# State-space scan of a decoder trunk: outputs channel-major in the two partition halves, with a cross-chunk decay matrix

## The chip, the cores and the metric

The kernel runs on one core of a Trainium2 chip. The metric is the device time of one execution in microseconds (us). The engines are TensorE (PE, with its weight loads as PEld), VectorE (DVE), ScalarE (ACT), GpSimd (POOL) and SyncE (SP), which issues the weight loads.

## The reference

The reference is a trunk of four pre-norm residual layers with 256 tokens of 1024 channels. Layers 0 and 3 mix tokens by latent attention, layer 1 by block attention, layer 2 by a Mamba-2 state-space mixer; each is followed by a squared-ReLU MLP. The change is in the mixer of layer 2, whose scan works in two chunks of 128 tokens:

```python
def ssd_scan(xh, dt, a, bm, cm):
    x_dt = chunks(xh * dt[..., None])
    a_cs = jnp.cumsum(chunks(dt * a), axis=2)
    ...
    cb = jnp.einsum('bclgn,bcsgn->bclsg', cc, bc)
    y_diag = jnp.einsum('bclsg,bclsgr,bcsgrp->bclgrp', cb, decay_in, x_dt)
    decay_out = jnp.exp(a_cs[:, :, -1:] - a_cs)
    states = jnp.einsum('bclgn,bclgr,bclgrp->bcgrpn', bc, decay_out, x_dt)
    ...
    y_off = jnp.einsum('bclgn,bcgrpn,bclgr->bclgrp', cc, prev, jnp.exp(a_cs))
    return (y_diag + y_off).reshape(B, S, *xh.shape[2:])
```

There are 32 heads of 64 channels in two groups of 16. `decay_in` is `exp(a_cs[l] - a_cs[s])` for s up to l, else 0. The output then gets the skip term, is gated by `silu(z)`, normalised per group and projected by `ssd_w_out`.

## The kernel before, in words

Every weight matrix is cut into units of up to 1 MB. SP fetches a unit into one of four slots (`raw`); ACT makes its rounded high part (`whi`, line 474) and DVE the rest (`wlo`, line 484). A product with a weight is three products of such parts (`mm3`, lines 501 to 503; in output projections lines 695, 696 and 699). `act_splits` and `dve_splits` say how far ahead of PE the splitting goes. Outputs of PE go to four PSUM banks in turn, handed out by `Jobs`: each job takes the next bank, and PE waits until the bank's previous user has been read. `acc` is four further banks for the output projections. Every engine executes its own list in the order of the code.

The mixer's stage (`pe_ssd`, `act_ssd`, `dve_ssd`, `pool_ssd`) has two parts. First ten convolution steps: PE projects 256 channels (`cv`), ACT copies them and starts the sum, DVE adds three taps (line 1471), ACT applies silu (line 1349); `xsT`, `BT` and `CT` hold the results channel-major. After step 4, `Btok` (the transposed B of chunk 0) and `cbm` (C times B, masked) are made. The scan loop then makes passes q = 0 to 4, of which 0 to 3 take eight heads each. In a pass PE:

- transposes `xsT` to token-major (`xT`, line 1295); DVE multiplies by dt (line 1543) into `xdt`, and by the decay to the chunk's end (line 1552) into `dxdt`;
- transposes the outputs of the pass before (`yT`, line 1304) back to channel-major, which DVE gates (`gate`, lines 1514 and 1520);
- projects two units of z (`z`, 2q and 2q+1), between them multiplies `Btok` by `dxdt` (`st`, line 1311), the state after chunk 0, copied to `prevT` by ACT;
- forms the products within chunks (`ydiag`, line 1273, called for both chunks), 16 products with `dec` as weights and 64 moving columns, and between them reads the state (`yo`, line 1316). ACT copies chunk 0's outputs to `y_sb`, DVE scales the state's part (line 1584) and adds (line 1590) for chunk 1;
- in some passes projects gated outputs (`pe_out`, units `so`): `out_units` gives so0 and so1 to pass 1, so2 and so3 to pass 2, so4 to so7 to pass 4.

`dec` is prepared one pass ahead: POOL fetches the cumulated sums of eight heads, spread over all partitions (`load`, line 1613), DVE subtracts each row's own sum (`diffs`, line 1484), ACT takes the exponential (`decays`, line 1383), DVE multiplies by `cbm` (`decay_cb`, line 1492). ACT holds one set of function tables at a time, so going from silu to the exponential and back costs a table load each.

Of the kernel before, what the change touches and what calls it, by code (L numbers as in the profile page):

```python
# [21 lines left out]
P = 128  # L22
# [80 lines left out]
def build(nc, A, out, stages):  # L103

    ctx = ExitStack()
    with ctx:
# [73 lines left out]
        tokv = sb("tokv", [P, 6, SSD_H])  # L180
# [42 lines left out]
        prevT = xn[:, 1, 512:1024]  # L223
        y_sb = junk[:].rearrange("p (c n) -> p c n", c=T)
        with ExitStack() as stage:
# [3 lines left out]
            Btok = sb("Btok", [P, SSD_G, P], F32, stage)  # L229
# [12 lines left out]
        if "ssd" in kinds:  # L242
            (ssd_loaded, upper_loaded, acs_stored, dt_abs, dt_exp, dt_u, dt_ln, dt_out, da_done, acs_done, dec_io,
             drows_done, conv_done, silu_done, dec_diff, dec_exp, dec_ready, dx_done, g_done, gsq_done, gadd_done,
             ghi_done, glo_done, gms_done, grstd_done, ssd_half, tokv_done) = (sem(n) for n in (
                 "ssd_loaded upper_loaded acs_stored dt_abs dt_exp dt_u dt_ln dt_out da_done acs_done dec_io "
                 "drows_done conv_done silu_done dec_diff dec_exp dec_ready dx_done g_done gsq_done gadd_done "
                 "ghi_done glo_done gms_done grstd_done ssd_half tokv_done").split())
# [119 lines left out]
        def plan_ssd(L):  # L368
# [4 lines left out]
            for n in range(10):  # L373
# [854 lines left out]
        DT, EXP, U, LN, DD, DEC, DTO, ACS = range(8)  # L1228

        def pe_ssd(te, j, L):  # L1230
# [12 lines left out]
            for n in range(10):  # L1243
                if n:
                    proj(("cv", n))
                if n == 4:
                    te.wait_ge(dt_out, 1)
                    te.wait_ge(acs_done, 1)
                    te.wait_ge(dec_io, 2)
                    ps = open_job(te, "tokv")  # L1250
                    for i, (row, c) in enumerate(((DTO, 0), (DTO, 1), (ACS, 0), (ACS, 1), (DEC, 0), (DEC, 1))):
# [11 lines left out]
                    ps = open_job(te, "Btok")  # L1263
                    for g in range(SSD_G):
                        mm = nc.tensor.transpose(ps[:, g * P:(g + 1) * P], BT[:, g, tok(0)], ident[:])
                    mm.then_inc(ready("Btok"), 1)
            job_copied(te, "Btok")
            def ydiag(q, c):
                te.wait_ge(dec_ready, 2 * q + c + 1)
                job_copied(te, ("xT", q, c))  # L1270
                ps = open_job(te, ("yd", q, c))
                for hh in range(8):
                    mm = nc.tensor.matmul(ps[:, hh * SSD_HD:(hh + 1) * SSD_HD], dec[:, (2 * q + c) % 4, hh, :],  # L1273
                                          xdt[:, c, hh * SSD_HD:(hh + 1) * SSD_HD], start=True, stop=True)
                mm.then_inc(ready(("yd", q, c)), 1)
# [11 lines left out]
            for q in range(5):  # L1287
# [9 lines left out]
                if q:  # L1297
                    job_copied(te, ("yd", q - 1, 0))
                    job_copied(te, ("yd", q - 1, 1))
                    for u in range(2):  # L1300
                        ps = open_job(te, ("yT", q - 1, u))
                        for i in range(2):
                            for c in range(T):
                                mm = nc.tensor.transpose(ps[:, i * SEQ + c * P:i * SEQ + (c + 1) * P],
                                                         y_sb[:, c, (2 * u + i) * P:(2 * u + i + 1) * P], ident[:])
                        mm.then_inc(ready(("yT", q - 1, u)), 1)
# [515 lines left out]
```

## Time and profile before

| | before |
|---|---|
| median of 3 runs | 1401.88 us (1400.38 to 1404.24) |
| profiled execution: time, span | 1399.73 us, 1397.8 us |
| mean granted TensorE clock | 0.983 |
| PE busy | 1332.3 us (95%), 8604 records |
| DVE busy | 857.0 us (61%) |
| ACT busy | 668.0 us (48%) |
| POOL busy | 40.5 us (3%) |

The span runs from the first to the last instruction. The share of busy time is an average over stages; the scan stage lies at about 660 to 870 us of the span. A matmul of fp32 operands has two records in the trace, a transpose one. A record's duration includes the time in which the next one has started, so what a product costs in a dense run is the distance between starts. The granted clock is 1.00 at 2.4 GHz and 0.50 at 1.2 GHz.

### The profile page before, as it was taken

How to read it: one execution, taken by the hardware profiler on the slowest of the kernel's cores; microseconds unless marked ns; L12 is line 12 of the kernel's file. 1: busy time of each engine (PE TensorE's matmuls, PEld its weight loads, DVE VectorE, ACT ScalarE, POOL GpSimd, SP SyncE). 2: the span in 40 equal slices, each digit the busy share in tenths (PEclk: the TensorE clock that was granted, in tenths of full speed). 3: DMA queues.
4: the chain of work that ended last, by engine and by line, in shares of the span. 5: the costliest groups of instructions: out<-in, count | busy, mean ns of one | idle time of the engine just before them, and what ended most of it. 6: DMA issues, size and time to landing. Idle time of an engine off the chain costs nothing.

```text
span 1397.8 us, 20308 instructions
## 1 busy us (share of the span) xinstructions
PE 1332.3 (95%) x8604; PEld 1211.0 (87%) x8604; DVE 857.0 (61%) x1125; ACT 668.0 (48%) x834; POOL 40.5 (3%) x59
## 2 busy tenths in 40 slices
PE   5899999999999899999997999999999999899997
PEld 5788789999899799998897997999988898799996
DVE  4777665554564665555798686655556776565553
ACT  4455454443455454443765553544434545544442
POOL 2000000000000000000101110000000000000000
PEclk9899999999999999999998999999998999999999
DMA  8654165556554365552773443755535233375540
GB/s 255 159 151 150 61 226 182 188 196 188 160 172 151 130 231 195 186 181 90 230 238 104 136 155 127 247 181 181 186 116 197 98 123 122 129 236 190 181 151 31
DMA packets 147834, 231.06 MB, mean 165 GB/s; under 512 B 7651, under 2 KB 116493, under 8 KB 147744
## 3 DMA queue, kind: packets, MB, share of 16 engines
q1 hardware_dynamic: 144896, 221.66, 48.5%
q0 software_dynamic: 2848, 8.10, 2.7%
q8 instruction: 69, 1.13, 0.3%
q14 instruction: 21, 0.17, 0.0%
HBM read 227.08 MB, written 2.65 MB: 164 GB/s over the span
## 4 chain that ended last, share of the span: by engine, by line
PE 83%; DVE 9%; ACT 4%; issue 2%; DMA 2%; POOL 0%; SPq 0%; DVEq 0%; POOLq 0%; ACTq 0%
PE bank L501 14%; PE bank L503 14%; PE bank L502 14%; PE acc L695 11%; PE acc L696 11%; PE acc L699 11%; DVE wlo L484 3%; PE bank L829 3%; ACT whi L474 2%; PE bank L847 1%; PE bank L630 1%; DMA raw<-in_mla_w_in 1%; DMA raw<-in_mla_w_ukv 1%; PE bank L837 1%; PE bank L1273 1%
## 5 line engine op out<-in xcount | busy, mean ns | idle before, releaser
L484 DVE TENSOR_TENSOR wlo<-raw,whi 128x2048 fp32r<-128x2048 f32 (+2 forms) x209 | 467.6, 2246 | 206.4 <-ACT whi L474 206.3
L474 ACT ACTIVATE whi<-raw 128x2048 fp32r<-128x2048 f32 (+2 forms) x209 | 388.7, 1870 | 92.3 <-PE acc L699 82.9
L501 PE MATMUL bank<-hhi,whi 128*128 128x256 f32 x1448 | 416.2, 287 | 11.2 <-DVE hlo L574 7.1
L502 PE MATMUL bank<-hlo,whi 128*128 128x256 f32 x1448 | 412.4, 285 | 0.0
L503 PE MATMUL bank<-hhi,wlo 128*128 128x256 f32 x1448 | 412.4, 285 | 0.0
L501 PEld LDWEIGHTS bank<-hhi,whi 128*128 128x128 f32 x1448 | 279.4, 193 | 17.3 <-DVE hlo L574 9.0
L502 PEld LDWEIGHTS bank<-hlo,whi 128*128 128x128 f32 x1448 | 279.5, 193 | 3.3 <-issue 1.0
L503 PEld LDWEIGHTS bank<-hhi,wlo 128*128 128x128 f32 x1448 | 279.5, 193 | 0.2
L696 PE MATMUL acc<-wlo,uhi 128*128 128x512 f32 x512 | 200.0, 391 | 0.0
L695 PE MATMUL acc<-whi,uhi 128*128 128x512 f32 x512 | 199.6, 390 | 0.0
L699 PE MATMUL acc<-whi,ulo 128*128 128x512 f32 x512 | 159.1, 389 | 0.0
L778 ACT ACTIVATE relu<-bank 128x512 f32<-128x512 f32 x64 | 38.2, 597 | 213.3 <-PE bank L503 213.3
L699 PEld LDWEIGHTS acc<-whi,ulo 128*128 128x128 f32 x512 | 96.1, 188 | 20.4
L791 DVE TENSOR_TENSOR rsq<-relu 128x512 f32<-128x512 f32 x64 | 44.2, 691 | 112.1 <-ACT relu L778 112.1
L696 PEld LDWEIGHTS acc<-wlo,uhi 128*128 128x128 f32 x512 | 96.4, 188 | 18.1
L695 PEld LDWEIGHTS acc<-whi,uhi 128*128 128x128 f32 x512 | 96.4, 188 | 18.0
L794 DVE TENSOR_TENSOR ulo<-rsq,uhi 128x512 fp32r<-128x512 f32 x64 | 44.3, 693 | 50.5 <-ACT uhi L782 50.5
L782 ACT ACTIVATE uhi<-rsq 128x512 fp32r<-128x512 f32 x64 | 40.5, 632 | 64.4 <-DVE rsq L791 55.6
L695 PE MATMUL acc<-whi,ohi 128*128 128x512 f32 x160 | 63.9, 399 | 0.8 <-issue 0.8
L696 PE MATMUL acc<-wlo,ohi 128*128 128x512 f32 x160 | 62.6, 391 | 0.0
L501 PE MATMUL bank<-whi,hhi 128*128 128x256 f32 (+1 forms) x160 | 47.7, 298 | 10.5 <-DVE wlo L484 6.7
L529 ACT ACTIVATE hhi<-bank 128x512 fp32r<-128x512 f32 x32 | 18.7, 598 | 81.6 <-PE bank L630 81.5
(213 smaller groups left out, 1664.7 us busy)
## 6 DMA issues: line engine op xcount, KB each, us to landing
raw<-in_mlp_w SPq DMA_DIRECT2D x128, 1024.0 KB, 5.3
raw<-in_ssd_w_in SPq DMA_DIRECT2D x18, 1024.0 KB, 6.1
raw<-in_mla_w_o SPq DMA_DIRECT2D x16, 1024.0 KB, 5.0
raw<-in_mla_w_ukv SPq DMA_DIRECT2D x8, 1024.0 KB, 7.6
raw<-in_moba_w_qkv SPq DMA_DIRECT2D x16, 512.0 KB, 6.7
raw<-in_ssd_w_out SPq DMA_DIRECT2D x8, 1024.0 KB, 5.0
raw<-in_mla_w_uq SPq DMA_DIRECT2D x8, 768.0 KB, 7.4
raw<-in_mla_w_in SPq DMA_DIRECT2D x4, 1024.0 KB, 7.6
```

Of the source, the lines that this page charges most:

```text
L474: nc.scalar.activation(whi[:, s, :e], raw[:, s, :e], ACT.Copy).then_inc(w_hi_done[s], 1)
L484: nc.vector.tensor_tensor(wlo[:, s, :e], raw[:, s, :e], whi[:, s, :e].bitcast(F32), ALU.subtract).then_inc(w_split[s], 1)
L501: nc.tensor.matmul(ps, lhs[0], rhs[0], start=start, stop=False)
L502: nc.tensor.matmul(ps, lhs[0], rhs[1], start=False, stop=False)
L503: return nc.tensor.matmul(ps, lhs[1], rhs[0], start=False, stop=stop)
L695: nc.tensor.matmul(acc[t][half][:], lh, wh[:, k, n], start=first_unit and k == 0, stop=False)
L696: nc.tensor.matmul(acc[t][half][:], lh, wl[:, k, n], start=False, stop=False)
L699: mm = nc.tensor.matmul(acc[t][half][:], ll, wh[:, k, n], start=False, stop=last_unit and k == 1)
L782: nc.scalar.activation(uhi[:, c % 2].rearrange("p a b -> p (a b)"), rsq[:, c % 2, :], ACT.Copy).then_inc(uhi_done, 1)
L791: nc.vector.tensor_tensor(rsq[:, c % 2, :], relu[:, c % 2, :], relu[:, c % 2, :], ALU.mult).then_inc(usq_done, 1)
L794: nc.vector.tensor_tensor(ulo[:, c % 2].rearrange("p a b -> p (a b)"), rsq[:, c % 2, :], uhi[:, c % 2].rearrange("p a b -> p (a b)").bitca ...
L829: mm = nc.tensor.matmul(dst, q[:, tok(t)], k[:, 0:(t + 1) * P], start=n == 0, stop=n == len(parts) - 1)
```

## The change

The state is gone. For eight heads a third tile beside the two of `dec`, called `cross`, holds the decay from the end of chunk 0 to each token of chunk 1, `exp(a_cs)` of chunk 1, times `cbx`, which is C of chunk 1 by B of chunk 0. It lies in `junk`; POOL fetches its sums (`load_cross`), ACT takes the exponential (`cross_decay`), DVE multiplies by `cbx` (`cross_cb`). The products are turned round: `xdt` and `dxdt` are the weights, 64 columns of one head each, and `dec` and `cross` move past them, so the result is channel-major and needs no transposing. The two heads of a pair go to partitions 0 to 63 and 64 to 127 of the same bank, and the cross product is added to chunk 1's in PSUM. `gate` reads that bank. Removed are `Btok`, `st`, `prevT`, `yo`, `y_sb`, `yT` and their copies.

The order also changes. The first `diffs`, `decays` and `decay_cb` go into the convolution steps 5, 7 and 8, with the first cross tile. `split_early` and `split_late` say which units are split where. DVE makes `dxdt` ahead of the gates. A pass has six jobs instead of ten; so the bank of `y` 2q is taken again by `z` 2q+2, and the job `ss` takes a bank out of turn.

```diff
-        prevT = xn[:, 1, 512:1024]
-        y_sb = junk[:].rearrange("p (c n) -> p c n", c=T)
+        cross = junk[:].rearrange("p (h n) -> p h n", h=8)
...
-            Btok = sb("Btok", [P, SSD_G, P], F32, stage)
+            cbx = sb("cbx", [P, SSD_G, P], F32, stage)
...
-                    jobs.add("Btok")
+                    jobs.add("cbx")
             for q in range(5):
                 if q < 4:
                     jobs.add(("xT", q, 0))
                     jobs.add(("xT", q, 1))
-                if q:
-                    jobs.add(("yT", q - 1, 0))
-                    jobs.add(("yT", q - 1, 1))
-                if q < 4:
...
-                        if u == 0:
-                            jobs.add(("st", q))
-                    jobs.add(("yd", q, 0))
-                    jobs.add(("yo", q))
-                    jobs.add(("yd", q, 1))
+                    jobs.add(("y", 2 * q))
+                    jobs.add(("y", 2 * q + 1))
                 if q in (2, 4):
-                    jobs.add(("ss", q // 2 - 1))
+                    turn = jobs.last
+                    jobs.add(("ss", q // 2 - 1), bank=(turn + 2) % 4)
+                    jobs.last = turn
...
+        so_of = {L: {n: ("so", L, n) for n in range(8)} for kind, L, i in stages if kind == "ssd"}
+        split_early, split_late = {}, {}
+        for so in so_of.values():
+            split_early = {0: ("z", 3), 1: ("z", 4), 2: so[3], 3: so[5]}
+            split_late = {0: so[1], 1: ("z", 5), 2: ("z", 7), 3: so[7]}
...
-                    ps = open_job(te, "Btok")
+                    ps = open_job(te, "cbx")
                     for g in range(SSD_G):
-                        mm = nc.tensor.transpose(ps[:, g * P:(g + 1) * P], BT[:, g, tok(0)], ident[:])
-                    mm.then_inc(ready("Btok"), 1)
-            job_copied(te, "Btok")
-            def ydiag(q, c):
-                te.wait_ge(dec_ready, 2 * q + c + 1)
-                job_copied(te, ("xT", q, c))
-                ps = open_job(te, ("yd", q, c))
...
+                        mm = nc.tensor.matmul(ps[:, g * P:(g + 1) * P], BT[:, g, tok(0)], CT[:, g, tok(1)],
+                                              start=True, stop=True)
+                    mm.then_inc(ready("cbx"), 1)
+            def scan(n):
+                q = n // 2
+                ps = open_job(te, ("y", n))
+                for i in range(2):
+                    hh = [4 * (n % 2) + 2 * i + a for a in range(2)]
+                    ch = [slice(h * SSD_HD, (h + 1) * SSD_HD) for h in hh]
+                    dst = [ps[a * SSD_HD:(a + 1) * SSD_HD, i * SEQ:(i + 1) * SEQ] for a in range(2)]
+                    for a in range(2):
+                        nc.tensor.matmul(dst[a][:, tok(0)], xdt[:, 0, ch[a]], dec[:, (2 * q) % 4, hh[a], :],
+                                         start=True, stop=True)
+                    for a in range(2):
+                        nc.tensor.matmul(dst[a][:, tok(1)], xdt[:, 1, ch[a]], dec[:, (2 * q + 1) % 4, hh[a], :],
+                                         start=True, stop=False)
+                    for a in range(2):
+                        mm = nc.tensor.matmul(dst[a][:, tok(1)], dxdt[:, ch[a]], cross[:, hh[a], :],
+                                              start=False, stop=True)
+                mm.then_inc(ready(("y", n)), 1)
...
-                if q:
...
                 if q < 4:
                     proj(("z", 2 * q))
+                    proj(("z", 2 * q + 1))
+                    job_copied(te, ("xT", q, 0))
+                    job_copied(te, ("xT", q, 1))
                     te.wait_ge(dx_done, q + 1)
-                    ps = open_job(te, ("st", q))
-                    nc.tensor.matmul(ps[:], Btok[:, q // 2, :], dxdt, start=True, stop=True).then_inc(ready(("st", q)), 1)
-                    proj(("z", 2 * q + 1))
-                    job_copied(te, ("st", q))
-                    ydiag(q, 0)
-                    ps = open_job(te, ("yo", q))
-                    nc.tensor.matmul(ps[:], CT[:, q // 2, tok(1)], prevT, start=True,
-                                     stop=True).then_inc(ready(("yo", q)), 1)
-                    ydiag(q, 1)
+                    te.wait_ge(dec_ready, 2 * (q + 1))
+                    te.wait_ge(cross_ready, q + 1)
+                    scan(2 * q)
+                    scan(2 * q + 1)
...
+            def cross_decay(q):
+                act.wait_ge(cross_loaded, 16 * (q + 1))
+                nc.scalar.activation(cross, cross, ACT.Exp).then_inc(cross_exp, 1)
...
+                if n == 7:
+                    decays(0)
+                    cross_decay(0)
...
-            decays(0)
             for q in range(5):
+                if q == 0:
+                    act_splits(act, ("z", 0))
                 if 0 < q < 4:
                     for n in (2 * q - 2, 2 * q - 1):
                         gate_square(n)
                         gate_hi(n)
+                    cross_decay(q)
                 if q == 4:
                     gate_square(6)
                     gate_square(7)
-                    act_splits(act, ("so", L, 4))
                     gate_hi(6)
                     gate_hi(7)
                 if q < 4:
                     for u in range(2):
                         n = 2 * q + u
-                        act_splits(act, ("z", n), AHEAD - 1)
                         ps = job_ready(act, ("z", n))
...
                         if u == 0:
-                            ps = job_ready(act, ("st", q))
-                            nc.scalar.activation(prevT, ps[:], ACT.Copy).then_inc(freed(("st", q)), 1)
-                    ps = job_ready(act, ("yd", q, 0))
-                    nc.scalar.activation(y_sb[:, 0, :], ps[:], ACT.Copy).then_inc(freed(("yd", q, 0)), 1)
-                    act_splits(act, ("z", 2 * q + 1))
+                            act_splits(act, split_early[q], 0)
                 if q < 3:
                     decays(q + 1)
-                for n in out_units[q]:
-                    act_splits(act, ("so", L, n), AHEAD - 1)
+                if q < 4:
+                    act_splits(act, split_late[q], 0)
+            act_splits(act, ("so", L, 7), AHEAD - 1)
...
+            def cross_cb(q):
+                dve.wait_ge(cross_exp, q + 1)
+                nc.vector.tensor_tensor(cross, cross, cbx[:, q // 2, :].unsqueeze(1).to_broadcast([P, 8, P]),
+                                        ALU.mult).then_inc(cross_ready, 1)
...
+                if n == 5:
+                    diffs(0)
+                if n == 8:
+                    job_copied(dve, "cb")
+                    job_copied(dve, "cbx")
+                    decay_cb(0, 0)
+                    decay_cb(0, 1)
+                    cross_cb(0)
...
-                ps = job_ready(dve, ("yT", n // 2, n % 2))
+                ps = job_ready(dve, ("y", n))
...
-                        dve.wait_ge(dx_done, q)
+                        dve.wait_ge(*jobs.at["y", 2 * q - 1][1])
                     for c in range(T):
...
-                if q:
-                    gate(2 * q - 2)
-                    gate(2 * q - 1)
-                if q < 4:
                     job_copied(dve, ("xT", q, 0))
                     nc.vector.tensor_tensor(dxdt.rearrange("p (h d) -> p h d", h=8),
                                             xdt[:, 0, :].rearrange("p (h d) -> p h d", h=8),
                                             tokv[:, 4, hs].unsqueeze(2).to_broadcast([P, 8, SSD_HD]),
                                             ALU.mult).then_inc(dx_done, 1)
-                if q == 0:
-                    diffs(0)
-                    decay_cb(0, 0)
-                    decay_cb(0, 1)
-                if q == 4:
-                    dve_splits(dve, ("so", L, 4))
+                if q:
+                    gate(2 * q - 2)
+                    gate(2 * q - 1)
...
+                if 0 < q < 4:
+                    cross_cb(q)
                 if q < 4:
-                    dve_splits(dve, ("z", 2 * q), AHEAD - 1)
-                    dve_splits(dve, ("z", 2 * q + 1), AHEAD - 1)
+                    dve_splits(dve, split_early[q], 0)
                     if q < 3:
                         diffs(q + 1)
...
-                    if q < 3:
                         decay_cb(q + 1, 0)
                         decay_cb(q + 1, 1)
-                    dve_splits(dve, ("z", 2 * q + 1))
+                    dve_splits(dve, split_late[q], 0)
                 if q == 2:
                     mean_square(0)
                 if q == 4:
                     mean_square(1)
-                for n in out_units[q]:
-                    dve_splits(dve, ("so", L, n), AHEAD - 1)
-                if q == 4:
+                    dve_splits(dve, ("so", L, 7), AHEAD - 1)
...
-                        pool.wait_ge(*jobs.at["yd", q - 2, c][1])
+                        pool.wait_ge(*jobs.at["y", 2 * q - 3][1])
                     src = acs_dram[8 * q:8 * q + 8, tok(c)].unsqueeze(0).to_broadcast([P, 8, P])
                     pool.dma_start(dec[:, b], src).then_inc(dec_loaded[b], 16)
+            def load_cross(q):
+                if q:
+                    pool.wait_ge(*jobs.at["y", 2 * q - 1][1])
+                src = acs_dram[8 * q:8 * q + 8, tok(1)].unsqueeze(0).to_broadcast([P, 8, P])
+                pool.dma_start(cross, src).then_inc(cross_loaded, 16)
...
+            load_cross(0)
...
+                if n % 2 == 0 and n < 6:
+                    load_cross(n // 2 + 1)
+                if n in (0, 2):
+                    load(n // 2 + 2)
...
-                if n in (1, 3):
-                    load(n // 2 + 2)
```

On DVE, at the end of the convolution and up to the first gate of pass 1, the kernel before has this order (lines of the kernel before: 1471 convolution taps, 484 weight split, 1543 and 1552 `xdt` and `dxdt`, 1484 subtractions, 1492 `decay_cb`, 1514 gate):

```order
L1471 SCALAR_TENSOR_TENSOR cacc<-cvin,scol,cacc 128x256 x6
L1543 TENSOR_TENSOR xn<-bank,tokv 128x512 x2
L1552 TENSOR_TENSOR xn<-xn,tokv 128x512
L1484 TENSOR_SCALAR dec<-dec,tokv 128x128 x16
L1492 TENSOR_TENSOR dec<-dec,cbm 128x1024 x2
L484 TENSOR_TENSOR wlo<-raw,whi 128x2048
L1484 TENSOR_SCALAR dec<-dec,tokv 128x128 x16
L1584 TENSOR_TENSOR junk<-bank,tokv 128x512
L1590 TENSOR_TENSOR junk<-bank,junk 128x512
L1492 TENSOR_TENSOR dec<-dec,cbm 128x1024 x2
L484 TENSOR_TENSOR wlo<-raw,whi 128x2048
L1543 TENSOR_TENSOR xn<-bank,tokv 128x512 x2
```

The changed kernel has (line 1472 taps, 1493 `decay_cb`, 1498 `cross_cb`, 479 split, 1556 and 1561 `xdt` and `dxdt`, 1485 subtractions, 1527 gate):

```order
L1472 SCALAR_TENSOR_TENSOR cacc<-cvin,scol,cacc 128x256 x6
L1493 TENSOR_TENSOR dec<-dec,cbm 128x1024 x2
L1498 TENSOR_TENSOR junk<-junk,cbx 128x1024
L479 TENSOR_TENSOR wlo<-raw,whi 128x2048
L1472 SCALAR_TENSOR_TENSOR cacc<-cvin,scol,cacc 128x256 x6
L1556 TENSOR_TENSOR xn<-bank,tokv 128x512 x2
L1561 TENSOR_TENSOR xn<-xn,tokv 128x512
L479 TENSOR_TENSOR wlo<-raw,whi 128x2048
L1485 TENSOR_SCALAR dec<-dec,tokv 128x128 x16
L1493 TENSOR_TENSOR dec<-dec,cbm 128x1024 x2
L479 TENSOR_TENSOR wlo<-raw,whi 128x2048 x2
L1556 TENSOR_TENSOR xn<-bank,tokv 128x512 x2
```

The first pass's multiplies now stand ahead of the last convolution step, and one more split stands ahead of pass 1's `xdt`.

On PE, between the end of pass 0's second z unit and pass 1's first, the kernel before has 16 products of `dec` around the read of the state, then two kinds of transposes:

```order
L1273 MATMUL bank<-xn,dec 128x64 x8
L1316 MATMUL bank<-xn,CT 128x512
L1273 MATMUL bank<-xn,dec 128x64 x8
L1295 MATMUL bank<-ident,xsT 128x128 x8
L1304 MATMUL bank<-ident,junk 128x128 x8
```

In the changed kernel the same place holds 24 products with 64 output partitions, each pair for the two halves, and one kind of transposes (the three rows stand four times):

```order
L1279 MATMUL bank<-dec,xn 64x128 x2
L1282 MATMUL bank<-dec,xn 64x128 x2
L1285 MATMUL bank<-junk,xn 64x128 x2
...
L1307 MATMUL bank<-ident,xsT 128x128 x8
```

The list gives a product once though the trace has two records of it.

## Rows read from the trace of the kernel before

**Rows 1.** The page's part 1 (busy time by engine) and part 4 (the chain):

```profile
PE 1332.3 (95%) x8604; PEld 1211.0 (87%) x8604; DVE 857.0 (61%) x1125; ACT 668.0 (48%) x834; POOL 40.5 (3%) x59
PE 83%; DVE 9%; ACT 4%; issue 2%; DMA 2%; POOL 0%; SPq 0%; DVEq 0%; POOLq 0%; ACTq 0%
```

**Rows 2.** Timeline of PE: start us, us, engine, line, operation, [idle before, releaser]:

```profile
759.84 0.55 PE L501 MATMUL bank<-hhi,whi 128*128 128x256 f32 x1 [3.78 <-DVE xn L1543]
...
774.81 1.90 PE L1273 MATMUL bank<-xn,dec 128*128 128x64 f32 x16
776.54 1.08 PE L1316 MATMUL bank<-xn,CT 128*128 128x512 f32 x2
777.46 1.89 PE L1273 MATMUL bank<-xn,dec 128*128 128x64 f32 x16
...
790.16 1.04 PE L1295 MATMUL bank<-ident,xsT 128*128 128x128 f32 x8
...
797.66 1.02 PE L1311 MATMUL bank<-xn,Btok 128*128 128x512 f32 x2
...
798.64 0.28 PE L502 MATMUL bank<-hlo,whi 128*128 128x256 f32 x1
...
820.51 1.04 PE L1295 MATMUL bank<-ident,xsT 128*128 128x128 f32 x8
...
840.06 1.06 PE L1304 MATMUL bank<-ident,junk 128*128 128x128 f32 x8 [0.90 <-issue]
840.88 0.48 PE L695 MATMUL acc<-whi,ghi 128*128 128x512 f32 x1
```

**Rows 3.** Timeline of DVE, last convolution steps and first two turns:

```profile
728.42 2.71 DVE L1471 SCALAR_TENSOR_TENSOR cacc<-cvin,scol,cacc 128x256 f32<-128x256 f32 x6 [0.84 <-ACT cacc L1361]
...
736.81 1.28 DVE L1543 TENSOR_TENSOR xn<-bank,tokv 128x512 f32<-128x512 f32 x2
738.01 0.68 DVE L1552 TENSOR_TENSOR xn<-xn,tokv 128x512 f32<-128x512 f32 x1
738.61 3.22 DVE L1484 TENSOR_SCALAR dec<-dec,tokv 128x128 f32<-128x128 f32 x16
742.73 2.36 DVE L1492 TENSOR_TENSOR dec<-dec,cbm 128x1024 f32<-128x1024 f32 x2 [0.90 <-ACT dec L1383]
...
756.81 2.28 DVE L484 TENSOR_TENSOR wlo<-raw,whi 128x2048 fp32r<-128x2048 f32 x1
759.01 1.28 DVE L1543 TENSOR_TENSOR xn<-bank,tokv 128x512 f32<-128x512 f32 x2
760.21 0.86 DVE L1514 SCALAR_TENSOR_TENSOR gy<-xsT,scol,bank 128x256 f32<-128x256 f32 x2
...
790.87 1.29 DVE L1543 TENSOR_TENSOR xn<-bank,tokv 128x512 f32<-128x512 f32 x2 [2.55 <-PE bank L1295]
```

**Rows 4.** Timeline of ACT in pass 0:

```profile
740.34 1.28 ACT L1383 ACT_TABLE_LOAD   x1 [2.78 <-DVE dec L1484]
741.63 2.01 ACT L1383 ACTIVATE dec<-dec 128x1024 f32<-128x1024 f32 x2
```

**Rows 5.** Stretches: us, busy us (records) by engine, granted clock, DMA share, GB/s:

```profile
689.50:722.60 33.10, 32.75 (x273) 32.20 (x272) 31.86 (x46) 24.23 (x33) 1.19 (x2) 1.00 0.90 278
755.00:758.00 3.00, 1.06 (x8) 0.66 (x6) 3.00 (x3) 0.00 (x0) 0.00 (x0) 0.56 0.02 5
864.70:868.10 3.40, 1.58 (x9) 0.95 (x8) 2.47 (x5) 0.60 (x1) 0.00 (x0) 0.99 0.00 0
868.10:871.50 3.40, 3.40 (x18) 3.40 (x17) 0.19 (x1) 0.15 (x1) 0.00 (x0) 0.51 0.56 159
```

**Rows 6.** Timeline of PE, last product on 32 weight columns and its successor:

```profile
669.42 0.41 PE L503 MATMUL bank<-hhi,wlo 128*32 128x256 f32 x1
669.64 0.81 PE L630 MATMUL bank<-ident,xn 128*128 128x128 f32 x4
```

**Rows 7.** DMA issues of the stage: KB each, median us to landing:

```profile
dec<-acs_rows POOLq DMA_DIRECT2D x8, 512.0 KB, 7.1
```

More of the change, by code:

```diff
@@ L179, in build @@
         headc = sb("headc", [SSD_H, 4])
-        tokv = sb("tokv", [P, 6, SSD_H])
+        tokv = sb("tokv", [P, 5, SSD_H])
         g_ms = sb("g_ms", [P, SSD_G, T])
@@ L244, in build @@
              drows_done, conv_done, silu_done, dec_diff, dec_exp, dec_ready, dx_done, g_done, gsq_done, gadd_done,
-             ghi_done, glo_done, gms_done, grstd_done, ssd_half, tokv_done) = (sem(n) for n in (
+             ghi_done, glo_done, gms_done, grstd_done, ssd_half, tokv_done, cross_loaded, cross_exp,
+             cross_ready) = (sem(n) for n in (
                  "ssd_loaded upper_loaded acs_stored dt_abs dt_exp dt_u dt_ln dt_out da_done acs_done dec_io "
                  "drows_done conv_done silu_done dec_diff dec_exp dec_ready dx_done g_done gsq_done gadd_done "
-                 "ghi_done glo_done gms_done grstd_done ssd_half tokv_done").split())
+                 "ghi_done glo_done gms_done grstd_done ssd_half tokv_done cross_loaded cross_exp cross_ready").split())
             dec_loaded = [sem(f"dec_loaded{b}") for b in range(4)]
@@ L1248, in pe_ssd @@
                     te.wait_ge(acs_done, 1)
-                    te.wait_ge(dec_io, 2)
+                    te.wait_ge(dec_io, 1)
                     ps = open_job(te, "tokv")
-                    for i, (row, c) in enumerate(((DTO, 0), (DTO, 1), (ACS, 0), (ACS, 1), (DEC, 0), (DEC, 1))):
+                    for i, (row, c) in enumerate(((DTO, 0), (DTO, 1), (ACS, 0), (ACS, 1), (DEC, 0))):
                         mm = nc.tensor.transpose(ps[:, i * SSD_H:(i + 1) * SSD_H], dtv[0:SSD_H, row, tok(c)],
@@ L1345, in act_ssd, with decays @@
             dst = [BT, CT] + [xsT[:, 2 * n:2 * n + 2, :] for n in range(ZT // 2)]
+            def decays(q):
+                for c in range(T):
+                    b = (2 * q + c) % 4
+                    act.wait_ge(dec_diff, 2 * q + c + 1)
+                    nc.scalar.activation(dec[:, b], dec[:, b], ACT.Exp).then_inc(dec_exp, 1)
+            def cross_decay(q):
+                act.wait_ge(cross_loaded, 16 * (q + 1))
+                nc.scalar.activation(cross, cross, ACT.Exp).then_inc(cross_exp, 1)
             def silu(n):
@@ L1365, in act_ssd @@
                     act.wait_ge(acs_done, 1)
-                    for i in range(2):
-                        ins = nc.scalar.activation(v[:, DEC, tok(i)], v[:, ACS, tok(i)], ACT.Exp,
-                                                   bias=v[:, ACS, P - 1:P] if i == 0 else 0.0,
-                                                   scale=-1.0 if i == 0 else 1.0).then_inc(dec_io, 1)
+                    nc.scalar.activation(v[:, DEC, tok(0)], v[:, ACS, tok(0)], ACT.Exp, bias=v[:, ACS, P - 1:P],
+                                         scale=-1.0).then_inc(dec_io, 1)
                 if n:
@@ L1372, in act_ssd @@
                 if n == 4:
-                    ps = job_ready(act, "Btok")
-                    nc.scalar.activation(Btok[:].rearrange("p a b -> p (a b)"), ps[:, 0:SSD_G * P],
-                                         ACT.Copy).then_inc(freed("Btok"), 1)
+                    ps = job_ready(act, "cbx")
+                    nc.scalar.activation(cbx[:].rearrange("p a b -> p (a b)"), ps[:, 0:SSD_G * P],
+                                         ACT.Copy).then_inc(freed("cbx"), 1)
+                if n == 7:
+                    decays(0)
+                    cross_decay(0)
             silu(9)
             act.wait_ge(silu_done, 10)
-            def decays(q):
-                for c in range(T):
-                    b = (2 * q + c) % 4
-                    act.wait_ge(dec_diff, 2 * q + c + 1)
-                    nc.scalar.activation(dec[:, b], dec[:, b], ACT.Exp).then_inc(dec_exp, 1)
             def gate_square(n):
```

28 lines of the change are left out of this document (3 added, 25 removed).

## The prediction

> **What bounds the kernel now.** I read the page first. TensorE (PE) is busy 95% of the span and carries 83% of the chain that ended last; VectorE (DVE) has 9% and ScalarE (ACT) 4% [rows 1]. So only what PE executes or waits for counts. PE's timeline of the scan loop [rows 2] places the change. The loop ends at 840.88 us, where the first of the last four units of the output projection starts. The reader should see that the passes are unlike: pass 2 is dense, 790.16 to 820.51 or 30.35 us, while ahead of pass 1 stands a hole of 3.78 us. DVE's and ACT's timelines [rows 3, 4] say why. After the last convolution step DVE works almost without a pause, and z2, the first projection of pass 1, starts at 759.84 only when DVE has run the first `xn` multiply at 759.01. From there to the 0.90 us ahead of the last `yT` no row of PE shows a wait. The granted clock [rows 5] is down to 0.56 in the stretch from 755 us, that is at 1.2 GHz in nearly all of it, behind PE's holes at this turn.
>
> **What PE gives up.** In a dense pass the records leave by their starts [rows 2]: the eight transposes of the outputs (`yT`), 0.82 us by 840.06 to 840.88; the state product, 0.86 us (797.66 to the second record of z5 at 798.64, less 0.12 for the first); the two blocks of diagonal products, 1.73 us before 776.54 and 1.70 us after 777.46; the read of the state, 0.92 us. That is 6.03 us per pass, 5.21 us without `yT`. At the end the 0.90 us hole and 0.82 us of `yT` before the last projections go too.
>
> **What PE gets: s per pass.** Twenty-four fp32 products with 64 weight columns and 128 moving columns, in two records each: 48 records. A record of 512 moving columns takes 0.46 us (the state read), a quarter of which is 0.115; the old products have 0.108 us each, 1.73 us over 16 records. One after the other, s = 48 x 0.108 = 5.2 us. But each pair writes the two halves of the partitions. If record two of one half runs beside record one of the other, s = 24 x 0.108 + 0.1 = 2.7 us. No row of this kernel shows two products at once, so these are the ends. I take 2.7 us, narrowly: the product that fills only 32 columns follows and is followed by full ones without a gap, 669.42 to 669.64 at 1.2 GHz [rows 6], so partial products bring no visible penalty. The Trainium skill (TensorEngine Tiling (Array Packing), Key Properties) says that tiles over different columns load weights and multiply in parallel, and that a change of tiling mode drains the engine. By its first half s is 2.7, by its second it is more, without a price. The page TensorE: Matmul & The Clock Gate of the same skill (Measured speedup vs the span model) gives 2.38 times for three column tiles; an estimate from it for two tiles is 1.6 times, s = 3.3 us and a sum of about zero. No row here bears on any of the three. The two replaced state transposes become two products of 0.2 us: nothing.
>
> **The turn into pass 1: +2.2 us.** Here the sum is a walk along two engines. DVE is saturated in the convolution (31.86 of 33.10 us busy [rows 5]). Into that go the 16 subtractions, 3.22 us, after step 5, and after step 8 two multiplies, 2.36 us, plus the new cross multiply, 1.2 us. ACT gets, after step 7, a table load of 1.28 us, exponentials of 2.01 us and a new one of 1.06 us, and the load back, 1.28 us [rows 4]. Step 6 of DVE then ends at about 722.7 instead of 719.5, ACT has its exponentials by 727.8, its next weight split by 729.7, so DVE ends step 8 at 734.6, the multiplies at 738.2 and step 9 at 743.1, instead of 736.8. PE hardly sees this: the scan operands are ready at 745.0, about when z1 ends. But next, DVE has 1.9 us of `xn` multiplies, the split of z3 behind ACT's (to 747.9), subtractions to 751.0, the multiplies behind ACT's exponentials to 754.2, and so0 and so1 (4.49 us), to 759.1. Only then `xn` (1.28), the scaled `xn` (0.68) and the first two gate operations (0.86). That matters since z2 now needs the bank of y0, which these two free; before it needed the bank of the transposes, free after one multiply. z2 starts at about 762.0, 2.2 us later. Whatever s is in pass 0, it is hidden under this wait.
>
> **The same bank wait in passes 2 and 3: +2.66 us each.** DVE is idle there when the transposes come. The multiply starts 0.71 us after them (790.16, 790.87), then 1.20, 0.61 and 0.86 us up to the second gate operation and 0.15 us to PE: z starts 3.53 us after the first transpose; the transposes take 0.87 us, so PE stands 2.66 us [rows 2, 3]. Other waits I cost at nothing: the cross tile is there 7.1 us after PE ends the previous pass [rows 7] and ACT wants it over 10 us later; DVE ends its cross multiply at 768 where the scan asks at 776. POOL's queue gets four loads more; the loads stand ahead of the sums of squares, which come later anyway. SP's weight loads wait for splits up to 6 us later, but of slots not read before 790. If that cover were gone, each pass would pay the late microseconds one for one. DVE's last work of pass 2 (to about 819) just fits before the transposes of pass 3.
>
> **The clock: 0 to +3.4 us.** At the end of the scan stage, short holes between transposes left PE busy 1.58 us of 3.40 from 864.7, and in the next 3.4 us the granted clock was 0.51 [rows 5]. Half speed for 3.4 us costs 1.7 us. The new holes of 2.66 us behind 0.87 us of transposes are as large. Ends: none, or both, 3.4 us; I take one, 1.7 us. In pass 1 it is low already, as before.
>
> **Sum.** Pass 1: +2.2 - 5.21 + s. Pass 2: -6.03 + 2.66 + s. Pass 3 and the end: -6.03 - 0.90 - 0.82 + 2.66 + s. Together -11.5 + 3s, and with the clock -9.8 + 3s. With s = 2.7 this is -1.7 us. The profiled execution took 1399.73 us (span 1397.8), so the changed one would take 1398.0; the median of the runs is 2.15 us above the profiled one, which gives **1400.2 us**.
>
> **Rivals.**
> 1. *The halves take turns.* Both columns of products share one stream, and s is 5.2 us. For it: every record in this trace follows its predecessor. Against: different partitions and weights. With none or both drops the sum is +4.1 to +7.5 us, 1406.0 to 1409.4 us, slower. It decides from s = 3.3 us on, where gain and loss are equal. Chance 0.38.
> 2. *DVE swallows the work in the convolution.* It waits 0.84 us in each of the last steps [rows 3]; if its real slack were larger, step 9 would end at 736.8 as before and z2 start 6.3 us sooner, giving 1393.9 us. Against: rows 5 leave 1.24 us of slack in 33.1, for 6.8 us of added work. Chance 0.12, and mostly part of the way.
>
> The forecast itself, halves side by side and DVE late, has 0.50: 1398.5 us if the clock never falls behind the new holes, 1401.9 us if it does so twice.
>
> **The numbers.** 0.3% is 4.2 us, about what a measurement of this kernel can tell from no change. Faster by more needs rival 2: 0.12. Slower by more is nearly all of rival 1: 0.38. Between: 0.50. The range reaches from part of rival 2, 1396 us, through the forecast to rival 1 with both drops, 1409.4 us, rounded to 1409.5; the forecast's own range is 1398 to 1402.5 us.
>
> **What would show it.** Twenty-four records' worth of time in a block of 48, or 48's; PE idle about 11 to 14 us ahead of z2, ended by the gate operation; z2 near 762 us; two holes of about 2.7 us ahead of z4 and z6, ended by the same line; the granted clock at 0.5 behind them or not. Holes elsewhere (ahead of the scan blocks, waiting for the cross tile) would make the prediction wrong, as would a z2 that starts before 756 us.

## Result and profile after

The changed kernel takes 1410.28 us (median of 6 runs, 1404.88 to 1411.54), the kernel before, in runs beside it, 1402.16 us (6 runs). The ratio is 1.0053, 95% interval 1.0035 to 1.0072: slower by 0.5%. Forecast were 1400.2 us and, as the likeliest case, no measurable change; the measured time lies outside the stated range of 1396 to 1409.5 us. The profiled execution took 1410.51 us, span 1408.7, mean granted clock 0.977 (before 0.983). Executions of one kernel differ by up to 8 us, and the time goes with the mean granted clock: of 71 of the kernel before, run beside the experiments, the 21 at 0.983 took 1398.3 to 1401.8 us and the 33 at 0.979 or less 1402.6 to 1406.6 us, so a few us between two profiled executions can be no effect of an edit.

The page's part 1 and the first line of part 4, which answer to [rows 1]:

```profile
PE 1330.9 (94%) x8621; PEld 1204.5 (86%) x8621; DVE 856.0 (61%) x1121; ACT 667.5 (47%) x829; POOL 41.8 (3%) x63
PE 85%; DVE 7%; ACT 4%; issue 2%; DMA 2%; POOL 0%; SPq 0%; DVEq 0%; POOLq 0%; ACTq 0%
```

PE is busy no longer than before, yet the span grew by 10.9 us. PE's timeline of the scan loop, answering to [rows 2] (starts in us; the stage's first and the next stage's first transposes are the first and last row):

```profile
666.78 1.03 PE L625 MATMUL bank<-ident,xn 128*128 128x128 f32 x8
...
739.18 1.04 PE L1307 MATMUL bank<-ident,xsT 128*128 128x128 f32 x8
...
754.42 1.09 PE L1307 MATMUL bank<-ident,xsT 128*128 128x128 f32 x8
768.27 0.55 PE L496 MATMUL bank<-hhi,whi 128*128 128x256 f32 x1 [12.76 <-DVE gy L1527]
...
782.45 0.28 PE L498 MATMUL bank<-hhi,wlo 128*128 128x256 f32 x1
782.66 0.44 PE L1279 MATMUL bank<-dec,xn 128*64 128x128 f32 x4
...
785.11 0.39 PE L1285 MATMUL bank<-junk,xn 128*64 128x128 f32 x4
785.43 0.51 PE L690 MATMUL acc<-whi,ghi 128*128 128x512 f32 x1
...
796.69 1.04 PE L1307 MATMUL bank<-ident,xsT 128*128 128x128 f32 x8
800.22 0.36 PE L496 MATMUL bank<-hhi,whi 128*128 128x256 f32 x1 [2.49 <-DVE gy L1527]
...
828.31 1.04 PE L1307 MATMUL bank<-ident,xsT 128*128 128x128 f32 x8
831.83 0.35 PE L496 MATMUL bank<-hhi,whi 128*128 128x256 f32 x1 [2.49 <-DVE gy L1527]
...
868.43 1.26 PE L625 MATMUL bank<-ident,xn 128*128 128x128 f32 x8
```

The local picture is the predicted one: 12.76 us idle ahead of z2, ended by the gate operation, a block of 48 records that starts at 782.66 and whose last four start at 785.11, 0.22 us for four (2.57 us from the first to the last start, about 2.7 us in all), and short holes of 2.49 us ahead of z4 and z6, ended by the same line. The whole stage takes 868.43 - 666.78 = 201.65 us. Before, it took 861.29 - 660.32 = 200.97 us; its transposes, those of pass 0, and those of the next stage were:

```profile
660.32 1.03 PE L630 MATMUL bank<-ident,xn 128*128 128x128 f32 x8
732.44 1.03 PE L1295 MATMUL bank<-ident,xsT 128*128 128x128 f32 x8
861.29 1.26 PE L630 MATMUL bank<-ident,xn 128*128 128x128 f32 x8
```

So of the 10.9 us only 0.7 lie in the stage that was changed, and the stage already starts 6.5 us late. The rest is in stages whose code is the same.

There one group of rows differs. By form, the products of the MLP's second projection, before:

```profile
L696 PE MATMUL acc<-wlo,uhi 128*128 128x512 f32 x512 | 200.0, 391 | 0.0
L695 PE MATMUL acc<-whi,uhi 128*128 128x512 f32 x512 | 199.6, 390 | 0.0
L699 PE MATMUL acc<-whi,ulo 128*128 128x512 f32 x512 | 159.1, 389 | 0.0
```

and after (busy us, mean ns of one):

```profile
L690 PE MATMUL acc<-whi,uhi 128*128 128x512 f32 x512 | 202.0, 394 | 0.0
L691 PE MATMUL acc<-wlo,uhi 128*128 128x512 f32 x512 | 201.6, 394 | 0.0
L694 PE MATMUL acc<-whi,ulo 128*128 128x512 f32 x512 | 162.1, 395 | 0.0
```

Their starts say what this is worth. One block of 24 in the first MLP, before:

```profile
304.35 0.40 PE L695 MATMUL acc<-whi,uhi 128*128 128x512 f32 x1
...
309.37 0.61 PE L699 MATMUL acc<-whi,ulo 128*128 128x512 f32 x2
315.57 0.40 PE L695 MATMUL acc<-whi,uhi 128*128 128x512 f32 x1
```

and after:

```profile
307.00 0.39 PE L690 MATMUL acc<-whi,uhi 128*128 128x512 f32 x1
...
312.11 0.63 PE L694 MATMUL acc<-whi,ulo 128*128 128x512 f32 x2
318.32 0.39 PE L690 MATMUL acc<-whi,uhi 128*128 128x512 f32 x1
```

From the first record of the block to the 23rd, 22 steps, it is 5.02 us before and 5.11 after, 228 and 232 ns per product; from block to block 11.22 and 11.32 us. The kernel has 2208 products with 512 moving columns on the split activations (three for each of 512, 160 and 64 groups). At 4.3 ns each, the mean difference of the three forms above and of the starts over the whole traces, that is 9.5 us. The products of 256 columns, 4344 of them, start every 120 ns in both.

What can change the pace of an instruction that is the same? Its addresses. The first line of the whole diff, which the excerpt above doesn't show, shortens a small table of the mixer by one of its six rows, the one that scaled the state's part:

```diff
-        tokv = sb("tokv", [P, 6, SSD_H])
+        tokv = sb("tokv", [P, 5, SSD_H])
```

This makes `tokv` 128 bytes per partition smaller. In the compiled programs' placement of tensors (bytes per partition) every tensor declared behind it moves down: `uhi` from 176768 to 176640, with `ulo`, `ohi`, `olo`, `ghi` and `glo`. The weights `whi` (49280) and `wlo` (82048) and the inputs `hhi`, `hlo` stay. From `whi` to `uhi` the distance was a multiple of 256 bytes (127488 = 498 x 256) and is now 128 off one.

### The profile page after: what moved, and what is told of

It is laid out like the page before. It is cut to its first block, busy times and chain, and to the rows that moved or that the text cites. A ratio compares the mean times of both kernels' runs of the same rounds, so it can differ in the third digit from the quotient of the medians.

```text
span 1408.7 us, 20324 instructions
## 1 busy us (share of the span) xinstructions
PE 1330.9 (94%) x8621; PEld 1204.5 (86%) x8621; DVE 856.0 (61%) x1121; ACT 667.5 (47%) x829; POOL 41.8 (3%) x63
## 4 chain that ended last, share of the span: by engine, by line
PE 85%; DVE 7%; ACT 4%; issue 2%; DMA 2%; POOL 0%; SPq 0%; DVEq 0%; POOLq 0%; ACTq 0%
PE bank L496 15%; PE bank L498 15%; PE bank L497 15%; PE acc L690 11%; PE acc L694 11%; PE acc L691 11%; PE bank L824 3%; DVE wlo L479 2%; ACT whi L469 2%; PE bank L842 1%; PE bank L625 1%; DMA raw<-in_mla_w_in 1%; DMA raw<-in_mla_w_ukv 1%; PE bank L832 1%; PE bank L843 1%
## 5 line engine op out<-in xcount | busy, mean ns | idle before, releaser
L694 PE MATMUL acc<-whi,ulo 128*128 128x512 f32 x512 | 162.1, 395 | 0.0
```

The lines of the kernel that those rows point to most:

```text
L694: mm = nc.tensor.matmul(acc[t][half][:], ll, wh[:, k, n], start=False, stop=last_unit and k == 1)
```

## Experiments

Theory A was that these addresses cost the 9 us; the rival B, that the new code itself (what it moves in time, or how instructions lie) slows the other stages. Four kernels tell them apart.

**tokv at its old size**, on the changed kernel:

```diff
-        tokv = sb("tokv", [P, 5, SSD_H])
+        tokv = sb("tokv", [P, 6, SSD_H])[:, 0:5, :]
```

> The changed kernel with tokv kept at its old size, so that every tensor behind it in SBUF lies 128 bytes higher, where it lay before. Nothing is left out. Theory A (the address of the operands sets the pace of the 512-column products of all projections): mean duration of these matmuls falls from 394 to 390 ns, some 2208 of them give back 4.7 ns each, 10 us, and the time is 1400 to 1402 us, within 0.3% of the kernel before. Rival B (the changed scan code itself, or how its instructions lie in memory, slows the other stages): durations stay at 394 and the time at about 1410.

Measured: 1401.62 us (12 runs), ratio to before 0.9998 (0.9984 to 1.0012). One line of declaration takes 8.7 us off the changed kernel by the medians, 7.7 us by the two ratios. The products are back, by form:

```profile
L691 PE MATMUL acc<-wlo,uhi 128*128 128x512 f32 x512 | 200.0, 391 | 0.0
L690 PE MATMUL acc<-whi,uhi 128*128 128x512 f32 x512 | 199.6, 390 | 0.0
L694 PE MATMUL acc<-whi,ulo 128*128 128x512 f32 x512 | 159.1, 389 | 0.0
```

**The kernel before, shifted**: the counter-test without any of the change.

```diff
+        sb("pad", [P, 32])
         g_ms = sb("g_ms", [P, SSD_G, T])
```

> The kernel before with 128 unused bytes per partition placed ahead of g_ms, so that uhi, ulo, ohi, olo, ghi and glo lie 128 bytes higher and the weights whi and wlo where they were. Theory A: the 512-column products take 394 ns instead of 390 and the kernel is 10 us slower, about 1412, with no change in its code. Rival B: no change, 1402.

Measured: 1409.49 us, ratio 1.0053 (1.0034 to 1.0072), the same as the change's own. By form:

```profile
L696 PE MATMUL acc<-whi,uhi 128*128 128x512 f32 x512 | 202.0, 394 | 0.0
L697 PE MATMUL acc<-wlo,uhi 128*128 128x512 f32 x512 | 201.6, 394 | 0.0
L700 PE MATMUL acc<-whi,ulo 128*128 128x512 f32 x512 | 162.0, 395 | 0.0
```

B falls: without any new code the kernel slows down as much. In both kernels the shift costs 7 to 9 us; the intervals reach to 10 us, so this can't be told from the 9.5 us of the sum.

**Half the shift** (a pad of `[P, 16]` at the same place, on the changed kernel), and **everything shifted** (the pad of `[P, 32]` ahead of `raw`, on the kernel before).

> The changed kernel with 64 unused bytes per partition ahead of g_ms: uhi and its neighbours lie half way between the two places. Theory A with a fine grain: something between 390 and 394 ns and between 1401 and 1410 us. Theory A with a coarse grain (only one of the places is good): 1410, as the changed kernel, or 1401, as with tokv at its old size. Rival B: 1410.

> The kernel before with 128 unused bytes per partition at the head of SBUF's tensors, so that weights and activations move together. If only the distance between the stationary and the moving operand counts, nothing changes: 390 ns and 1402 us. If each one's own address counts, the 512-column products take 394 ns and the kernel 1412 us. Rival B: 1402.

With the half shift: 1403.51 us, ratio 1.0007 (0.9992 to 1.0022), means 391, 391 and 392 ns: between the two, nearer to the good one. With weights and activations moved together: 1403.52 us, ratio 1.0007 (0.9991 to 1.0024), means 390, 391 and 389 ns. So it isn't where `uhi` lies by itself but how far it lies from the tensors declared ahead of it. Theory A takes this for the distance to the stationary operand, `whi` or `wlo`. The runs don't isolate that pair: `raw`, `x` and `xn` kept their distance to the weights in all of them, and ScalarE and VectorE write and read `raw`, `whi` and `wlo` while TensorE works. A shift of the weights alone would tell.

**hhi and hlo shifted** asks whether the 256-column products feel it too; on the changed kernel the pad also takes `uhi` back to its old place. It bears on the open point too, since `hhi`, `hlo`, `ident` and `junk` now lie 128 bytes nearer to `uhi` than in the kernel before.

```diff
+        sb("pad", [P, 32])
         hhi = sb("hhi", [P, KD, SEQ], F32R)
```

> The changed kernel with 128 unused bytes per partition ahead of hhi: hhi and hlo then lie 128 bytes off the distance to whi and wlo that they had, while uhi, ohi and ghi are back at the place that they had in the kernel before. The 512-column products should be at 390 ns. Theory A in its wide form (the distance of stationary and moving operand slows every matmul): the 4344 products of 256 columns on hhi and hlo, 120 ns apart until now, slow down by up to 4.7 ns each, 20 us, and the time is about 1421. Narrow form (only products of 512 columns feel it): they stay 120 ns apart, 1402.

Measured: 1401.95 us, ratio 0.9997 (0.9985 to 1.0009); the mean of the first of the three products is 284 ns instead of 287. The timeline shows a new rhythm with the same mean:

```profile
309.79 0.28 PE L499 MATMUL bank<-hhi,wlo 128*128 128x256 f32 x1
309.91 0.28 PE L497 MATMUL bank<-hhi,whi 128*128 128x256 f32 x1
310.02 0.28 PE L498 MATMUL bank<-hlo,whi 128*128 128x256 f32 x1
310.14 0.28 PE L499 MATMUL bank<-hhi,wlo 128*128 128x256 f32 x1
310.27 0.28 PE L497 MATMUL bank<-hhi,whi 128*128 128x256 f32 x1
```

Three steps take 0.36 us (309.91 to 310.27), as they do unshifted at 120 ns each. The wide form of A is out; the narrow one stands, and this run is a second kernel with the change whose 512-column products are near their old pace (means 391, 390 and 390 ns) and whose time is that of before. So the distance from `uhi` to `hhi`, `hlo`, `ident` and `junk` isn't what counts.

The other experiments take the kernel with the old `tokv` (1401.62 us) as their base and test the local steps. **The halves in turn**:

```diff
-                for i in range(2):
...
-                    for a in range(2):
+                for a in range(2):
+                    for i in range(2):
```

> The changed kernel with tokv at its old size (as in the first run here, 1401.62 us), and in scan(n) all products of the lower half of the partitions ahead of all of the upper half, instead of alternating; the same 24 matmul records with the same operands. Theory (neighbouring records of the two halves run side by side): a block of 48 records takes 5.2 us instead of 2.65, in passes 1 to 3 the whole of it is on TensorE's path and in pass 0 it lies ahead of a wait for VectorE, so 3 x 2.55 = 7.7 us more, about 1409. Rival (a record costs 55 ns whatever its neighbour, since 64 columns of the weights load faster): no change, 1402.

Measured: 1408.21 us, ratio 1.0038 (1.0023 to 1.0052), so 6.6 us more than the base. A block takes 4.04 us from its first to its last start against 2.57 in the base, so a record's neighbour does matter and the rival is out. But one after the other would be 5.1 us (47 steps of 109 ns), and the timeline shows why it is less (the upper half's products on `dec` are again lines 1279 and 1281):

```profile
777.07 0.43 PE L1279 MATMUL bank<-dec,xn 128*64 128x128 f32 x2
777.34 0.38 PE L1281 MATMUL bank<-dec,xn 128*64 128x128 f32 x2
...
777.78 0.38 PE L1279 MATMUL bank<-dec,xn 128*64 128x128 f32 x2
778.00 0.27 PE L1281 MATMUL bank<-dec,xn 128*64 128x128 f32 x1
778.00 0.32 PE L1279 MATMUL bank<-dec,xn 128*64 128x128 f32 x1
```

Two records in line take 0.22 us, 109 ns each: that is the price alone. At each turn from one half to the other the next half's records start while the last ones of this half still run (two starts at 778.00). Three such turns per block save the missing 1.1 us, and the three blocks on PE's path cost 4.4 us and not 7.7. In this profile the clock stayed at 1.00 behind both short holes, where the base fell; so its stage is only 0.2 us longer than the base's and its execution 3.7 us. Three of its ten executions, this one among them, had a mean clock of 0.982 and took 1403.6 to 1405.0 us, the other seven 0.973 to 0.975 and 1407.0 to 1411.0 us. How the medians' 6.6 us divide stays open.

**The banks**: z in the banks of the transposes from pass 1 on.

```diff
-                    jobs.add(("xT", q, 0))
-                    jobs.add(("xT", q, 1))
+                    jobs.add(("xT", q, 0), bank=0 if q else 2)
+                    jobs.add(("xT", q, 1), bank=1 if q else 3)
...
-                        jobs.add(("z", n), ready=used(("z", n)))
+                        jobs.add(("z", n), bank=u, ready=used(("z", n)))
```

> The changed kernel with tokv at its old size, and with z(2q), z(2q+1) in the PSUM banks of xT(q,0), xT(q,1) for q from 1 on, so that they wait for VectorE's xdt alone and not for the gate operations on y. Theory (the bank of y is what z waits for): z2 starts 2.1 us sooner, the holes of 2.5 us ahead of z4 and z6 shrink by about 1.9 us each, and the clock no longer falls behind them (2 x 1.7 us): 9.3 us less, 1392, or 1396 if the clock falls still. Rival (the holes come from something else that ends at the same time, the weights of z4 and z6): 1401, holes ended by another releaser.

Measured: 1395.64 us, ratio 0.9954 (0.9937 to 0.9971): 6.0 us less. Pass 2's turn:

```profile
789.57 1.04 PE L1307 MATMUL bank<-ident,xsT 128*128 128x128 f32 x8
791.11 0.36 PE L496 MATMUL bank<-hhi,whi 128*128 128x256 f32 x1 [0.51 <-DVE xn L1556]
```

The hole is 0.51 us, ended by the multiply of `xn`, and the clock no longer falls. The base has behind its hole, and this kernel has not (stretches: us, busy us by engine, granted clock, DMA share, GB/s; the base first):

```profile
795.10:798.60 3.50, 3.50 (x20) 3.50 (x20) 2.79 (x4) 2.36 (x6) 2.21 (x2) 0.56 0.00 0
```

```profile
791.10:796.00 4.90, 4.89 (x41) 4.90 (x42) 4.83 (x8) 1.43 (x3) 1.29 (x1) 1.00 0.02 5
```

z4 and z5 take 11.5 us from first to last start here and 12.9 in the base: 1.5 us for each fall of the clock. The wait ahead of z2 fell by 2.0 us, as expected. The medians show less than the 9.3 us expected, though PE's rows of the scan passes give nearly all of it (8.7 us by their starts); the other stages of this execution took 4.7 us longer than the base's.

**The turn**: VectorE's `diffs(1)`, `decay_cb(1)` and the splits of so0 and so1 behind the gates.

```diff
                     gate_lo(2 * q - 1)
+                if q == 1:
+                    diffs(1)
+                    decay_cb(1, 0)
+                    decay_cb(1, 1)
+                    dve_splits(dve, split_late[0], 0)
```

(with `decays(1)` moved behind `gate_hi` on ScalarE)

> The changed kernel with tokv at its old size, and between pass 0 and pass 1 the diffs(1), decay_cb(1) and the splits of so0 and so1 on VectorE put behind the gates of y0 and y1 (on ScalarE the decays(1) too). Theory (VectorE's queue, 13 us of it, is what keeps z2): TensorE's wait ahead of z2 falls from 13 us to 3 us, 10 us less, 1392. Rival (the transfers are the bound there, since the DMA share is 0.94 to 1.05 from 750 to 762 us): TensorE starts z2 sooner and waits behind for the weights of z3 to z5 or so0, time 1397 to 1402.

> Both edits, the banks and the turn, on the changed kernel with tokv at its old size. Theory: z2 starts within 1.5 us of the end of xT1's transposes, 12 us sooner, and the two short holes and their clock drops go, 7 us more: 1383 us. Rival (the transfers bound this stretch): 1390 to 1397, with waits of TensorE for the splits of weights.

The turn alone: 1397.65 us, ratio 0.9971 (0.9957 to 0.9985), 4.0 us less, not 10; in its profile the stage is 6.7 us shorter. PE's waits from 720 to 870 us in that kernel (total, times, longest):

```profile
PE bank L496 <- DVE gy L1529: 7.5, 3, 2.5
PE bank L1279 <- DVE junk L1500: 4.8, 1, 4.8
```

The 12.8 us ahead of z2 are 2.5, as the theory had it, but 4.8 us come back at another place: scan(2) waits for the cross tile, whose multiply stands behind 4.5 us of splits on VectorE. No wait is for weights, so the rival named the wrong culprit. Both edits together: 1391.01 us, ratio 0.9918 (0.9902 to 0.9935), where 1383 was expected; the time is the rival's, but again no wait is for weights. It is the same new wait, at 6.7 us:

```profile
751.65 0.36 PE L496 MATMUL bank<-hhi,whi 128*128 128x256 f32 x1 [0.51 <-DVE xn L1558]
...
770.11 0.70 PE L1279 MATMUL bank<-dec,xn 128*64 128x128 f32 x4 [6.71 <-DVE junk L1500]
770.56 0.67 PE L1282 MATMUL bank<-dec,xn 128*64 128x128 f32 x4
```

Behind it the granted clock is 0.50 from 770.0 to 775.0 us and the records of the block run at half speed, 0.43 us for four instead of 0.22. **The last edit** puts `cross_cb(1)` ahead of the splits:

```diff
                     decay_cb(1, 1)
+                    cross_cb(1)
                     dve_splits(dve, split_late[0], 0)
...
-                if 0 < q < 4:
+                if 1 < q < 4:
                     cross_cb(q)
```

> The last kernel (banks and turn) with cross_cb(1) ahead of the splits of so0 and so1 on VectorE. Theory (scan(2) waits 6.7 us for cross_cb(1), which stands behind 4.5 us of splits; its decays come ready 1 us later than the splits start): TensorE waits 2 to 2.5 us ahead of scan(2) instead of 6.7, the clock falls for less long, and the time is 4 to 6 us less, 1385 to 1387. Rival (so0 is then late, since its split starts 1.2 us later): the wait comes back ahead of so0 and the time is 1390.

```profile
768.48 0.44 PE L1279 MATMUL bank<-dec,xn 128*64 128x128 f32 x4 [2.31 <-DVE junk L1500]
```

The wait fell to 2.31 us as expected, and so0 wasn't late. Measured: 1389.54 us, ratio 0.9901 (0.9884 to 0.9917). That is 1.5 us below the last kernel (by the ratios 2.4 us, each against the kernel before beside it), where 4 to 6 were expected, and the intervals overlap, so the medians don't show a gain; the scan passes are 5.5 us shorter by PE's starts (31.13 us from the second to the third pair of transposes against 36.60), but other stages of this execution took longer. The lowest median of the study, it is 13.2 us below the kernel before beside it.

## Why the prediction was wrong, point by point

- **What failed is the step "Sum"**: it adds terms of the scan stage alone to the profiled 1399.73 us and so takes the other stages as unchanged. It passed over the first line of the diff. The term for the rest of the kernel was nothing, without a reason given. The runs put 8.7 us there (1410.28 against 1401.62 with the old `tokv`), more than any single term of the sum, and the kernel before pays about the same for the same shift (7 us). With that line undone the changed kernel is at 1401.62 us, inside the forecast's own range of 1398 to 1402.5, so its case of no measurable change would have held. In part that would have been luck, as the last point here shows: the stage's terms were off in both directions.
- **s, taken as 2.7 us**: 2.7 measured (2.57 us from the first to the last start and 0.11 for the last pair). The halves run side by side; alone a record takes 109 ns, in pairs 55 ns. The doubt was put at a chance of 0.38 for rival 1; it isn't what made the kernel slower, though the time, 1410.3, looks like its case. The Trainium skill's page TensorEngine Tiling (Array Packing), Key Properties, says that different tiles can multiply in parallel, and the trace agrees. Of the draining that it states for a change of mode the trace may show this: from the last projection record to the first scan record it is 0.21 us (782.45 to 782.66) where neighbours stand 0.12 apart, and from the last four scan records to the next projection 0.32 us (785.11 to 785.43) where four take 0.22, so 0.1 us on each side of a block. That this is the draining was not tested. The prediction's estimate of 1.6 times for two tiles, from the page TensorE: Matmul & The Clock Gate of the Trainium skill (Measured speedup vs the span model), is 2.0 here, 109 against 55 ns.
- **The turn into pass 1, +2.2 us**: z2 starts 29.09 us after the pass-0 transposes (739.18 to 768.27). From the profile of before this was 27.40, so +1.7. VectorE's last convolution step ends 10.0 us behind these transposes, 4.4 before: its queue took the work as forecast (the last step's end is the start of the first `xn` multiply). Rival 2 is out.

```profile
749.18 1.28 DVE L1556 TENSOR_TENSOR xn<-bank,tokv 128x512 f32<-128x512 f32 x2
```

- **The bank wait, 2.66 us twice**: 2.49 twice, and the bank experiment brought it to 0.51 by a change of banks.
- **The clock, taken as one fall, 1.7 us**: it fell behind both holes, 1.5 us each, 3.0 in all. Stretches of the changed kernel behind the holes ahead of z4 and z6 (columns as above):

```profile
801.70:805.20 3.50, 3.50 (x19) 3.50 (x18) 2.80 (x4) 2.35 (x6) 2.20 (x2) 0.51 0.00 0
833.30:837.00 3.70, 3.70 (x24) 3.70 (x23) 2.99 (x6) 3.23 (x7) 1.73 (x2) 0.65 0.01 2
```

z4 and z5, and z6 and z7, take 12.9 us from first to last start; with a hole of 2.5 us and no fall (the halves in turn) they take 11.5. So a hole of this size doesn't always bring the fall.

- **The sum of the stage**, -1.7 us: +0.7 measured. Of the 2.4 us between, 1.3 are the second fall, some 0.8 the stage's own 192 slower products (192 x 4.3 ns), some 0.5 the 0.1 us on each side of three blocks, and 0.3 the convolution, whose end comes that much later. Against them stand 0.5 at the turn and 0.3 at the bank waits; about 0.3 us stay open. With the old `tokv` the stage takes 201.02 us (660.40 to 861.42), 0.05 more than before: the 6 us of records per pass did go, and 2.7 us of new records per pass, the waits for a bank and the clock took them back. The bank and turn edits get 12 us out of it with the same products.

## To carry to other kernels

Read a diff for what it does to the placement of tensors, not only for its instructions: a buffer that shrinks moves all that are declared behind it, and when a kernel slows down in stages whose code didn't change, compare the mean durations of equal instructions there before looking for waits. When an edit removes work from the bounding engine, follow who frees the bank or buffer for its next step; here the saved time came back as a wait for a bank that one line of the plan could avoid. Where a wait goes, look in the helping engine's queue for what is asked for next: after the first move the cross tile's multiply was last in line.

## What the runs showed of the hardware

- The pace of products of fp32r operands (the rounded format of the split parts) with 512 moving columns depends on the distance in SBUF from the weights, and what lies with them, to the moving operand: 228 ns at a multiple of 256 bytes, 232 ns at 128 off one, in between at 64; not on the moving operand's address itself (moved together with the weights by 128 bytes, it keeps 228 ns). That the stationary operand is the partner isn't shown apart from `raw`, `x` and `xn`. Products of 256 columns keep their mean of 120 ns and only change their rhythm. By what mechanism was not tested.
- Products on 64 weight columns in the two halves of the partitions overlap even where the program lists one half's before the other's, for a few records at each turn: 4.04 us from the first to the last start of 48 records, against 2.57 alternating.
- Behind a hole of 2.49 us in TensorE's work the granted clock fell to 0.5 and cost 1.5 us, in the changed kernel at both short holes; with the halves in turn it didn't fall behind either, and behind holes of 0.51 us it didn't.
